# The modulation vectors of a two-block transformer kernel: from VectorE products to TensorE strips of 32 columns

## The reference

```python
sh, sc, gt = jnp.split(jax.nn.silu(c) @ w_ada[l] + b_ada[l], 3, axis=-1)
sh_c, sc_c, gt_c = jnp.split(jax.nn.silu(c_ctx) @ w_ada[l] + b_ada[l], 3, axis=-1)
h = rms_norm(x, norm_g[l]) * (1 + sc[:, None]) + sh[:, None]
hc = rms_norm(ctx, norm_g[l]) * (1 + sc_c) + sh_c
... = split_proj(h @ w_in[l])      # and hc @ w_in[l]; then three kinds of attention
x = x + gt[:, None] * (concatenate([ya, yb, yn]) @ w_out[l])   # layer 0: ctx likewise
```

## Time and profile before

| | us |
|---|---|
| median of 3 runs | 1351.19 (1347.23 to 1355.54) |
| the profiled execution | 1344.85 |
| its span, first to last instruction | 1343.1 |

### The profile page before, as it was taken

One profiled execution on the slowest core, in us unless ns is written; L12 is line 12 of the kernel. 1 busy time (PEld: TensorE's weight loads), 2 busy tenths in 40 slices (PEclk: granted clock), 3 DMA queues, 4 the chain that ended last, 5 costly groups with the idle time before them and its releaser, 6 DMA issues.

```text
span 1343.1 us, 16785 instructions
## 1 busy us (share of the span) xinstructions
PE 1172.3 (87%) x5909; PEld 944.0 (70%) x5909; DVE 752.7 (56%) x1361; ACT 607.7 (45%) x1178; POOL 253.0 (19%) x323
## 2 busy tenths in 40 slices
PE   1678698889897898689998899898969999999987
PEld 1656466667676677567786678787858888888875
DVE  2756558578675174455445455665456565555543
ACT  2043233434566154345447454344454445544553
POOL 5017214024500412230230012100012221111100
PEclk9998888989899798899999989998989999999999
DMA  7627725333310332312220276454526665444401
GB/s 180 203 63 217 149 69 137 97 109 109 94 64 17 82 110 79 95 48 63 79 79 16 88 261 188 157 158 140 184 84 206 185 184 162 127 124 126 141 2 47
DMA packets 79475, 158.63 MB, mean 118 GB/s; under 512 B 5910, under 2 KB 6206, under 8 KB 79136
## 3 DMA queue, kind: packets, MB, share of 16 engines
q1 hardware_dynamic: 74992, 145.82, 35.1%
q0 software_dynamic: 4400, 11.73, 4.0%
HBM read 154.39 MB, written 3.78 MB: 118 GB/s over the span
## 4 chain that ended last, share of the span: by engine, by line
PE 68%; DVE 10%; ACT 8%; DMA 5%; POOL 4%; issue 4%; SPq 0%; ACTq 0%; POOLq 0%; DVEq 0%
PE bank L635 16%; PE bank L636 16%; PE bank L637 16%; PE bank L762 4%; DMA raw<-in_w_ada_dram 4%; PE bank L737 3%; PE bank L747 3%; PE bank L837 2%; DVE work L1514 2%; POOL small L1352 2%; DVE w_lo L1492 2%; PE bank L810 2%; ACT w_hi L933 2%; PE bank L822 1%; PE bank L655 1%
## 5 line engine op out<-in xcount | busy, mean ns | idle before, releaser
L635 PE MATMUL bank<-w_lo,h_hi 128*128 128x512 f32 (+1 forms) x1152 | 469.2, 407 | 46.9 <-DVE h_lo L1562 16.4
L636 PE MATMUL bank<-w_hi,h_lo 128*128 128x512 f32 (+1 forms) x1152 | 453.9, 394 | 0.0
L637 PE MATMUL bank<-w_hi,h_hi 128*128 128x512 f32 (+1 forms) x1152 | 452.6, 393 | 0.0
L1492 DVE TENSOR_TENSOR w_lo<-raw,w_hi 128x1024 fp32r<-128x1024 f32 x224 | 285.0, 1278 | 292.2 <-ACT w_hi L933 290.6
L933 ACT ACTIVATE w_hi<-raw 128x1024 fp32r<-128x1024 f32 x224 | 236.2, 1058 | 313.3 <-PE bank L637 260.8
L635 PEld LDWEIGHTS bank<-w_lo,h_hi 128*128 128x128 f32 x1152 | 227.0, 197 | 102.8 <-issue 32.5
L637 PEld LDWEIGHTS bank<-w_hi,h_hi 128*128 128x128 f32 x1152 | 226.1, 196 | 46.2
L636 PEld LDWEIGHTS bank<-w_hi,h_lo 128*128 128x128 f32 x1152 | 227.1, 197 | 41.1 <-issue 0.2
L1514 DVE SCALAR_TENSOR_TENSOR work<-raw,cvec,work 128x512 f32<-128x512 f32 x138 | 98.0, 763 | 31.4 <-DMA raw<-in_w_ada_dram 31.1
L762 PE MATMUL bank<-work,stage 128*128 128x128 f32 x640 | 93.5, 288 | 1.5 <-ACT stage L1118 1.3
L1109 ACT ACTIVATE stage<-bank,small 128x512 f32<-128x512 f32 (+1 forms) x96 | 57.1, 598 | 71.4 <-DVE small L1709 71.3
(11 more groups left out here) (161 smaller groups left out, 1139.9 us busy)
## 6 DMA issues: line engine op xcount, KB each, us to landing
raw<-in_b_w_in_dram SPq DMA_DIRECT2D x80, 512.0 KB, 3.6
raw<-in_w_in_dram SPq DMA_DIRECT2D x56, 512.0 KB, 3.7
raw<-in_w_ada_dram SPq DMA_DIRECT2D x48, 512.0 KB, 3.8
raw<-in_a_w_in_dram SPq DMA_DIRECT2D x48, 512.0 KB, 4.0
raw<-in_w_out_dram SPq DMA_DIRECT2D x16, 512.0 KB, 3.5
raw<-in_a_w_out_dram SPq DMA_DIRECT2D x16, 512.0 KB, 3.6
raw<-in_b_w_out_dram SPq DMA_DIRECT2D x8, 512.0 KB, 3.5
work<-bias POOLq DMA_DIRECT2D x24, 96.0 KB, 4.4
```

The costliest lines, as they stand in the source:

```text
L635: pe.matmul(bank, hT(h_hi, ph, kt, tt), w_lo[:, s, k, lo:lo + w], start=first, stop=False)
L636: pe.matmul(bank, hT(h_lo, ph, kt, tt), w_hi[:, s, k, lo:lo + w], start=False, stop=False)
L637: mm = pe.matmul(bank, hT(h_hi, ph, kt, tt), w_hi[:, s, k, lo:lo + w], start=False, stop=last)
L1492: dve.tensor_tensor(w_lo[:, i % SPLIT, :, :], raw[:, PIECE_AT[p] % RAW, :, :], w_hi[:, i % SPLIT, :, :].bitcast(F32), ALU.subtract).then_i ...
```

## The change

New tiles come in place of the partial sums. `cpad` holds both vectors padded with zeros to 32 columns for each of the eight row blocks. A matmul with `cpad[:, kt]` as weights and 128x512 of `w_ada` as moving data, in plain f32, writes two used rows and 30 zero rows into one strip of 32 PSUM partitions, at partition 32 * (kt % 4).

1. At the start the 16 pieces have places of their own (`ada_first`, in memory that the first heads use later), a semaphore each, and SP issues them without any wait: chunks 0 and 1, then x, then chunks 2 and 3, then the first three pieces of `in0`, then the context. PE makes eight matmuls a chunk (`ada_row`), DVE copies the bank (`ada_keep_row`), and four matmuls with the two columns `pick` (ones at the used rows) add the four strips and turn the rows into columns (`ada_columns`).
2. Beside `in0`, PE makes four matmuls, one in each strip, when two pieces are there (`ada_half`, after the attention step of the chunk's second and fourth piece, in the bank that the transposes use), and DVE copies or adds the bank (`ada_add`). A piece's slot is free only when the pair has been used. `ada_total` has four matmuls with two columns in place of eight with one; for the gates it is one matmul for each vector, as before. The same goes for the last 8 pieces.
3. In `in0` and `in1`, in the first and last piece of a chunk after the first, PE runs the tiles outermost; ACT takes the head transpose before its last tile, and its attention step comes after all four tiles.
4. In ACT's and DVE's order at the start, the squares and the normalising of the context tiles come later, behind the first weight pieces.

```diff
+ADA_HALF = {p: (*was[:2], was[2] // 2) for p, was in ADA_BESIDE.items() if was[2] % 2}
-PIECES = (ada_pieces(0, range(4)) + first_pieces() + ada_pieces(1, (4, 5)) + pieces_of("out0") + pieces_of("in1")
+PIECES = (first_pieces() + ada_pieces(1, (4, 5)) + pieces_of("out0") + pieces_of("in1")
...
-            return ada_own.seen(p) if ada_own_piece(p) else ada_vector.seen((*p, 1, ada_whos(*p[:2])[-1]))
+            return ada_products_made.seen((*p[:2], p[2] // 2))
...
+            for p in ada_pieces(0, range(2)):
+                sp.dma_start(ada_first[:, p[1], p[2], :, :], weight_source(p)).then_inc(*ada_landed[p].at(p))
+            sp.dma_start(x[:, 0:2, :], a["x"][0].rearrange("(t p) d -> p t d", p=P)).then_inc(*start_loads["x"].at(0))
+            for p in ada_pieces(0, (2, 3)):
+                sp.dma_start(ada_first[:, p[1], p[2], :, :], weight_source(p)).then_inc(*ada_landed[p].at(p))
...
+            def ada_row(j):
+                bank = take(pe, SCORE_BANKS[j % 2], "ada_row", j)
+                for p in ada_pieces(0, (j,)):
+                    pe.wait_ge(*ada_landed[p].seen(p))
+                    for k in range(2):
+                        kt = 2 * p[2] + k
+                        g = 32 * (kt % 4)
+                        mm = pe.matmul(bank[g:g + 32, :], cpad[:, kt, :], ada_first[:, j, p[2], k, :], start=(kt < 4), stop=(kt >= 4))
+                mm.then_inc(*ada_products_made.at(j))
...
+            def ada_half(name, j, half):
+                bank = take(pe, TURN_BANK, "ada_half", name, j, half)
+                for pair in (2 * half, 2 * half + 1):
+                    pe.wait_ge(*landed[PIECE_AT[(name, j, pair)] % RAW].seen((name, j, pair)))
+                for kt in range(4 * half, 4 * half + 4):
+                    g = 32 * (kt % 4)
+                    mm = pe.matmul(bank[g:g + 32, :], cpad[:, kt, :], raw[:, PIECE_AT[(name, j, kt // 2)] % RAW, kt % 2, :], start=True, stop=True)
+                mm.then_inc(*ada_products_made.at((name, j, half)))
...
                         weights(p)
-                        for k in range(2):
+                        if len(tts) == 4 and n in (0, pairs - 1):
                             for tt in tts:
-                                product(ph, c, p, k, tt)
-                            tt = TURNED_AFTER.get((n, k))
-                            if c and tt in tts:
-                                head_turn(ph, c - 1, tt)
-                            if k == 0 and after_piece:
-                                after_piece((p, 0))
+                                for k in range(2):
+                                    product(ph, c, p, k, tt)
+                                if tt % 2 and c and (n, tt // 2) in TURNED_AFTER:
+                                    head_turn(ph, c - 1, TURNED_AFTER[(n, tt // 2)])
+                        else:
+                            by_half(ph, c, p, n, after_piece)
...
             pe.wait_ge(*setup_v.seen("cpad"))
+            ada_row(0)
+            ada_row(1)
+            ada_columns(0)
+            ada_row(2)
+            ada_columns(1)
             norm_turns("in0", 0)
+            ada_row(3)
+            ada_columns(2)
+            ada_columns(3)
...
-                for k in range(2):
-                    for who in ada_whos(name, j):
-                        to, w, c = ada_place(name, j)[:, who, :], raw[:, slot, k, :], cvec[:, 2 * pair + k, who:who + 1]
-                        if pair == first and k == 0:
-                            dve.tensor_scalar(to, w, c, None, ALU.mult).then_inc(*ada_vector.at((*p, k, who)))
-                            continue
-                        dve.wait_ge(*ada_vector.seen((*p, 0, who) if k else (name, j, pair - 1, 1, who)))
-                        dve.scalar_tensor_tensor(to, w, c, to, ALU.mult, ALU.add).then_inc(*ada_vector.at((*p, k, who)))
```

More of the change, by code:

```diff
@@ L396, in freed @@
                 return ada_kept.seen(rest)
+            if kind == "ada_row":
+                return ada_row_made.seen(rest[0])
+            if kind == "ada_half":
+                return ada_added.seen(rest)
             if kind == "score":
@@ L571, in _ @@
             ring = [0]
-            def ada_own_products(j):
-                p = ("ada0", j, 0)
-                bank = take(pe, (TURN_BANK, OUT_BANK)[j % 2], "ada", "ada0", j)
-                pe.wait_ge(*landed[PIECE_AT[p] % RAW].seen(p))
-                for k in range(2):
-                    for i in range(4):
-                        mm = pe.matmul(bank[:, 2 * i:2 * i + 2], raw[:, PIECE_AT[p] % RAW, k, i * P:(i + 1) * P], cvec[:, k, :],
-                                       start=(k == 0 and i == 0), stop=False)
-                mm.then_inc(*ada_own.at(p))
@@ L584, in ada_total @@
-            def ada_total(name, j):
-                if j < 4:
-                    own = ada_at_start(name, j)
-                    bank = bank_of("ada", name, j) if own else take(pe, TURN_BANK, "ada", name, j)
-                    pe.wait_ge(*ada_used((name, j, 3)))
-                    for i in range(4):
-                        for who in range(2):
-                            mm = pe.matmul(bank[:, 2 * i + who:2 * i + who + 1], ada_place(name, j)[:, who, i * P:(i + 1) * P], ones[:, 0:1],
-                                           start=(i == 0 and who == 0 and not own), stop=(i == 3 and who == 1))
+            def ada_row(j):
[7 more added lines that the diff above has]
+                mm.then_inc(*ada_products_made.at(j))
@@ new lines, in ada_columns @@
+            def ada_columns(j):
+                bank = take(pe, j, "ada", "ada0", j)
+                pe.wait_ge(*ada_row_made.seen(j))
+                for i in range(4):
+                    mm = pe.matmul(bank[:, 2 * i:2 * i + 2], ada_rows[j % 2][:, i * P:(i + 1) * P], pick, start=(i == 0), stop=(i == 3))
+                mm.then_inc(*ada_summed.at(("ada0", j)))
+            def ada_half(name, j, half):
[6 more added lines that the diff above has]
+                mm.then_inc(*ada_products_made.at((name, j, half)))
@@ L594, in ada_total @@
+            def ada_total(name, j):
+                pe.wait_ge(*ada_added.seen((name, j, 1)))
+                if j < 4:
+                    bank = take(pe, TURN_BANK, "ada", name, j)
+                    for i in range(4):
+                        mm = pe.matmul(bank[:, 2 * i:2 * i + 2], ada_sum[:, i * P:(i + 1) * P], pick, start=(i == 0), stop=(i == 3))
                     mm.then_inc(*ada_summed.at((name, j)))
                     return
-                pe.wait_ge(*ada_used((name, j, 3)))
@@ L597, in ada_total @@
                 for who in ada_whos(name, j):
                     bank = take(pe, (TURN_BANK, OUT_BANK)[who], "ada", name, j, who)
-                    pe.matmul(bank[:, :], ones[:, :], ada_place(name, j)[:, who, :], start=True, stop=True).then_inc(*ada_summed.at((name, j, who)))
+                    pe.matmul(bank[:, :], spread[:, who, :], ada_sum[:, :], start=True, stop=True).then_inc(*ada_summed.at((name, j, who)))
             turned = set()
@@ L706, in project, with by_half @@
                         between(c)
+            def by_half(ph, c, p, n, after_piece):
+                tts = tiles_of(ph)
+                for k in range(2):
+                    for tt in tts:
+                        product(ph, c, p, k, tt)
+                    tt = TURNED_AFTER.get((n, k))
+                    if c and tt in tts:
+                        head_turn(ph, c - 1, tt)
+                    if k == 0 and after_piece:
+                        after_piece((p, 0))
             def attention1(layer):
@@ L778, in step @@
                     for task in fill.get(i, ()):
+                        if task[0] == "half":
+                            ada_half(*task[1:])
                         if task[0] == "y":
@@ L1165, in _ @@
             split_until(SPLIT)
-            for tt in ALL_TILES[1:]:
-                norm_tile("in0", tt)
+            act.wait_ge(*start_loads["ctx"].seen(0))
+            for tt in CTX_TILES:
+                for half in range(2):
+                    square("in0", tt, half)
+                norm_tile("in0", tt - 1)
+            norm_tile("in0", 3)
             act.wait_ge(*setup_v.seen("lambda_sums"))
@@ L1556, in norm_tile @@
                 ins.then_inc(*scaled_v.at((ph, tt)))
-                if tt + 2 in tiles_of(ph):
+                if ph != "in0" and tt + 2 in tiles_of(ph):
                     normalise(ph, tt + 2)
@@ L1760, in step @@
                     for task in tasks:
-                        if task[0] == "products":
-                            ada_products(task[1])
+                        if task[0] == "half":
+                            ada_add(*task[1:])
                         if task[0] == "y":
@@ L1804, in _ @@
             for tt in ALL_TILES[1:]:
+                if tt - 1 in X_TILES:
+                    normalise("in0", tt + 1)
                 norm_tile("in0", tt)
```

100 lines of the change are left out of this document (55 added, 45 removed).

## The result

The changed kernel takes 1318.5 us (median of 4 runs, 1317.1 to 1321.4); the kernel before, run beside it, 1352.0 us (4 runs, 1347.2 to 1355.5). The ratio is 0.976, interval 0.972 to 0.979: faster by 2.4%, 33.5 us. The forecast was 1328 us, 1305 to 1350. In the profiled executions the gain is smaller: 1344.85 us before (span 1343.1), 1321.37 after (span 1319.6), 23.5 us, because that execution of before lies at the low end of its runs and that of after at the high end of its own.

What follows compares the result with a forecast made beforehand. Start bound by a load-and-slot ring, most of `in0` by PE, the remaining attention by a chain over all engines. Terms -15.5 - 5 - 5 + 2 = -23.5 us from 1344.85 give 1321; median 6.3 higher: 1328 us, 1305 to 1350.

Steps and rivals of the forecast that it cites:

- The start: Before the first product: loads without slot waits land by 44 us, first product at 56, gain 17 us.
- Chunk 0: First chunk of `in0`: later context squares and normalising delay tile 1 by 1.5 us (0 to 3).
- A group of strips: Beside `in0`: four matmuls in column strips overlap, 1.15 us a group, 13.8 us for 12 groups on PE.
- Rivals 1 and 2: Strip groups: strips don't overlap, 36 us, 1364, chance 0.12; or weight loads stand between them, 24 us, 1352, chance 0.08.
- The sums saved: `ada_total` beside `in0`: 16 passes (3.55 us) fall to 8 in four chunks, -7.1 us on PE.
- Waits on DVE's sums: PE in `in0`: of 9.9 us waiting for DVE's part of the modulation sums, 7 go.
- Added wait 1: Chunks 1 and 2 of `in0`: PE waits for both pieces of a pair, +6 us (0 to +12).
- Rival 3: Chunks 1 and 2 of `in0`: pairs hold slots and stall weight loads, 12 and 8 us, 1342, chance 0.15.
- Added wait 2: `ada_half` waits for ACT to free the transposes' bank: costed at nothing, 1 us allowed in each of 12 groups.
- Chunk ends: Tile-outer order removes bank waits: -13 us in `in0` with clock, +2 for ACT's later step, -5 in `in1`.
- The rest of the attention: Behind `in0`, 343 to 449 us: four strip groups on PE, less DVE work, +2 us (-2 to +5).
- Rival 4: Beside `in0`: DVE limits more than PE's waits tell, so a further 20 us come back, 1308, chance 0.15.

Runs made afterwards that it cites:

- e5: The changed kernel with DVE making the products beside `in0` and in the rest of the attention, new start and tile order kept: 1316.5 us, ratio 0.975.
- e6: The kernel before with the tile-outer order at chunk ends alone: 1334.6 us, ratio 0.987.
- e1: The kernel before with the new start alone, products beside `in0` on DVE and old tile order: 1333.0 us, ratio 0.988.
- e8: The changed kernel with the bias tables' small transfers one to two chunks later: 1315.2 us, ratio 0.973.
- e2: The changed kernel with the old tile order and ACT step at chunk ends, strips kept: 1335.5 us, ratio 0.990.
- e9: The changed kernel with chunk 1's pairs multiplied one piece later and the bias tables' transfers later: 1311.9 us, ratio 0.972.
- e10: e5 with the bias tables' transfers later: 1305.3 us, ratio 0.967.

## Why the prediction was right, and where its terms were off

The direction and the two large terms were right: the gain comes from the start and from the chunk ends, and taking 98 us of products off DVE is worth nothing by itself. The sum against the profiled execution, -23.5 us, was met to the tenth; that is luck, for its terms missed in both directions, and between the medians the gain is 33.5 us.

**The start.** Forecast: last landing at 44 us, first product at 56, gain 17. Measured 43.9 and 52.2, gain 20.6. The load sum (4.2 + 8.1 + 28.8 us and the landing) was right to 0.1 us. Over 8 to 40 us I expected DMA above 0.9 busy; the window of that stretch has 1.01. Mis-sized was the path from the landing to `a_scale`: 3.3 us in place of 6. I costed a small sum pass at 0.22 us, from the earlier trace rows, where 16 of them took 3.55 us; here 16 took 1.95 us. Of the same line eight passes took 1.87 us at 32.5 us, the cost that I had taken, so it is not the form that differs. By the timeline PE has hardly paused from 34.6 us on here; in the kernel before it had idled 17.4 us ahead of the matmuls that stand in front of the 16:

```profile
30.93 3.57 PE L580 MATMUL bank<-cvec,raw 128*128 128x2 f32 x16 [17.40 <-DMA raw<-in_w_ada_dram]
```

The rest is the way from `a_scale` to the first product, 5.0 us where I had 5.7.

**Chunk 0.** Forecast +1.5, measured +0.8. The granted clock in it is 0.92 where it was 1.00: PE idled from 47 to 52 us before it.

**A group of strips.** 1.15 us forecast, 1.07 measured at the full clock, 1.93 us where PE had stood before and the clock was granted at 0.50. Rivals 1 and 2 fall. The weight loads, by the view of line L604 (ns min/median/max):

```profile
L604 PEld LDWEIGHTS bank<-raw,work x128: 106/109/153, 109.2 to 355.8; 128*32 128x32 f32 x128
```

Eight passes of 0.43 us in a row would be 3.4 us. Four strips side by side leave 2 x 0.43 = 0.86 us, and eight loads of 109 ns between the passes would make that 1.7; measured are 1.07, so the strips run side by side and most of the loads is hidden behind them. Rows of the kernel before could have told the second half: its products follow each other 0.23 us apart with a load of 0.19 us for each. The sentence of the Trainium skill on row groups (TensorE: Matmul & The Clock Gate, Part 3: Packing small matmuls), taken to the letter, does not describe this case, where only the column group differs; its factor for column strips, 2.38 for three, is borne out in kind: four gave 3.62 / 1.07 = 3.4.

**The sums saved, mis-sized.** I took 16 passes of `ada_total` at the 3.55 us of the earlier trace rows, a row of the start, and -7.1 us in four chunks. In `in0` of the kernel before three of the four took half of that, for instance

```profile
247.19 1.84 PE L592 MATMUL bank<-ones,work 128*128 128x1 f32 x16
```

and only the one at 350.6 us, at a granted clock of 0.50, took 3.57. From its start to the next instruction a sum takes 1.77 us there (3.43 in the last) and 0.9 in the changed kernel, so 5.2 us are saved. The 12 groups cost 9 x 1.0 + 3 x 1.86 = 14.6 us where I had 13.8. The net is +9.4 us on PE for my +6.7.

**Waits on DVE's sums.** I counted 7 of 9.9 us as gone. In `in0` 8.6 us on `ada_cols` and L1568 are left (4.7 + 3.9) where the earlier trace rows has 9.9: `ada_keep` and the bias step still stand behind other work of DVE. This term was nearly nothing, and with it goes the last gain that the move beside `in0` had to its name.

**Added wait 1, mis-sized.** Forecast +6 us in chunks 1 and 2 together, 0 to 12. Chunk 1 alone is 15.3 us longer, PE waits 12.4 and 10.4 us, and chunk 2 gives back 5.3 (the second pair was then already done): +10 in all, inside the bounds. The places were right, second and fourth piece of chunk 1. I had seen PE standing from 116.5 to 126.6 us and from 143 to 151, 18 us, and counted two thirds of it as lost before too. The waits are 22.8 us, a little more, and what failed is the second half: the products of the next piece stand behind the group in PE's order, and only chunk 2's 5.3 us come back. How much of the 10 us is owed to the strips is open: the same two chunks took 87.8 to 89.2 us in e5, e6 and e1, whose products are DVE's as before, and against e5 the strips add 5.3. What these kernels share with the changed one is the late load. Its piece was there 14.8 us after its issue in the kernel before, 14.7 in the changed one, 18.3, 19.0 and 20.5 in e5, e6 and e1; why it varies is not shown. The earlier start does not make it, for e6 has the old start. Of the 22.8 us of waiting, 12.7 go when the small transfers go (e8). Rival 3 named this mechanism with a price of 20 us in place of my 6; the truth lies between, and far from the 1342 us of the rival.

**Added wait 2.** Costed at nothing. By the view of line L604 the groups waited for ACT's copy out of the transposes' bank 1.2 us in all, five times:

```profile
ACT stage L1156: 1.2, 5
```

Held.

**Chunk ends, and the rest of `in0`.** Forecast -13 + 2 in `in0` and -5 in `in1`, -16 us in all. Runs with this edit alone: -15.4 (e6), -16.5 (e5 against e1), -17 (against e2). I had left 3 us of waits on the banks; 0.4 are left. Right in the medians, and the best term of the sum. Its parts are less sure. The 4 us of clock that I gave back are not to be seen: e6 has 0.89, 0.95 and 0.91 in chunks 3 to 5 where 0.89, 0.95 and 0.92 was granted before. And e2 loses the 17 us with only half of the waits back. That -5 of it falls in `in1` fits the shorter in1 stretch of the profiled execution, some 5 us. Chunks 3 to 5 are each 1.3 to 3.4 us shorter; I had said 2 to 5 each. Chunks 1 to 6 together, from 85.7 us to the last product of chunk 6:

```profile
85.70:325.60 239.90, 204.39 (x968) 147.79 (x969) 104.76 (x207) 91.07 (x217) 84.06 (x90) 0.91 0.45 124
```

239.9 us for the 237.5 of before, where the sum had -5 and I had named 240 as the point from which I am wrong. The last product itself ends at 326.4 us, and at 343.7 in the kernel before: 240.7 for 238.2, past the point. So by my own sign this part of the forecast was wrong: `in0` behind chunk 0 missed by nearly 8 us, all of it in chunk 1, and the start and the median made up for it.

**The rest of the attention.** Forecast +2, -2 to +5. From the end of the last product of `in0` to `out0` it took 104.7 us where it was 105.4: -0.7, inside the bounds.

**Rival 4, DVE more of a limit.** It falls most clearly. DVE has 53 us less to do in e9 than in e10 and the stretch is 7.0 us longer; of the 12.4 us that PE has more to do, more than half shows in the time.

**The median.** I added 6.3 us to the profiled sum because the profiled execution of before lay below its median. The changed kernel's profiled execution lay 2.8 us above its median. Together with the rounding that is the 9.5 us between 1328 and 1318.5. It need not be all scatter, for the medians of the runs with single parts of the change show a term of the sum too high: start and chunk 0 were forecast at -15.5 us and gave -16.6 (e1), the chunk ends at -16 and gave -15.4 to -17, but the strips beside and behind `in0` at 6.7 - 7 + 6 + 2 = +7.7 us, and they cost +2.0 (against e5) and +2.6 (e2 against e1). By the profiled executions the parts of that term came out higher than forecast, not lower. The two views don't agree, and which share of the 9.5 us is scatter stays open. What is shown is that strips and DVE's products stood in the same stall, and that without it the kernel with strips is 6.7 us slower.

## What to carry to other kernels

An engine that is half idle gives nothing back when its work is moved to one that is full: here 12.4 us more of PE's time made the stretch 7.0 us longer, and DVE's 53 us were worth nothing. As an upper bound, cost such a move at its full length on the engine that the page shows as full. Ask of every late load who waits for it now and who will wait after the change: the fourth modulation piece took 14.8 us to come in the kernel before as well, where DVE waited for it; with the strips PE did, 10.4 us, and 12.4 us more for the second piece. Two small shifts in order removed both. Judge a move only after the shared stall is cured: with the late load in place the two ways of making the products looked equal (1316.5 and 1318.5 us), without it they were 6.7 us apart.

## What the runs showed of the hardware

Four matmuls of 32 columns into four column strips of one bank run at once: four matmuls of 512 columns, two passes each in the trace, took 1.07 us (3.62 us in one strip). Sums of two columns cost 0.12 us a pass where PE had been at work (16 in 1.95 us) and 0.23 us earlier (8 in 1.87 us at 32.5 us, behind a stretch with waits for the loads); in both stretches the profile prints a granted clock of 1.00, so at the start of a kernel the length of the passes tells more than that column. A load of 512 KB, 3.8 us in the median of the earlier trace rows, took 14.6 us while 319 packets of small transfers with 0.37 MB held 50% of the engines' time; with these transfers later, PE's wait for it, 10.4 us, was gone.
